# Three operands turned on VectorE and through HBM instead of on TensorE

## The reference, cut to what matters

```python
# hgrn2_chunkwise is the recurrence, h the normed tokens
o_a = rmsnorm(hgrn2_chunkwise(...), hg_norm_g) * silu(g_a)      # the recurrence's gated output
y_a = o_a @ w_branch_a
o_b = fox_attention(...)
y_b = o_b @ w_branch_b
y = gate[:, :, 0] * y_a + gate[:, :, 1] * y_b                   # the mixer's output
x = x + rmsnorm(y @ w_out, mix_post_g)
mem_n = rmsnorm(mem, mem_kv_g)                                  # the memory, normed
k, v = split(mem_n @ w_mkv)
x = x + rmsnorm(mem_cross_attention(rmsnorm(x, mem_pre_g), mem_n, ...), mem_post_g)
```

## Time and profile before

| | |
|---|---|
| median of 3 runs | 1068.75 us (1068.25 to 1068.9) |
| profiled execution | 1069.21 us |
| its span | 1067.2 us |
| PE busy | 1057.5 us, 99% |
| DVE busy | 737.4 us, 69% |
| ACT busy | 596.3 us, 56% |
| HBM read and written | 211.57 MB and 14.68 MB |

### The profile page before, as it was taken

One profiled execution on the slowest core, in us unless ns is written; L12 is line 12 of the kernel. 1 busy time (PEld: TensorE's weight loads), 2 busy tenths in 40 slices (PEclk: granted clock), 3 DMA queues, 4 the chain that ended last, 5 costly groups with the idle time before them and its releaser, 6 DMA issues.

```text
span 1067.2 us, 13290 instructions
## 1 busy us (share of the span) xinstructions
PE 1057.5 (99%) x5158; PEld 889.7 (83%) x5158; DVE 737.4 (69%) x868; ACT 596.3 (56%) x804; POOL 96.1 (9%) x73
## 2 busy tenths in 40 slices
PE   8999999999999999999999999999999999999997
PEld 6888888888888888888888888888989988888886
DVE  5668787785786666467986768657668665867642
ACT  6473677764384645548755545464356557655441
POOL 1900000000000000000545500010000000000000
PEclk9999999999999999999999999999999999999999
DMA  9754899985587777565457844366556346777851
GB/s 351 281 195 158 294 285 307 298 265 195 180 274 247 241 238 233 165 223 180 159 161 225 243 152 158 131 243 218 175 182 216 119 132 218 237 244 240 242 166 40
DMA packets 82831, 227.13 MB, mean 213 GB/s; under 512 B 9377, under 2 KB 28753, under 8 KB 82641
## 3 DMA queue, kind: packets, MB, share of 16 engines
q1 hardware_dynamic: 79344, 214.86, 61.7%
q0 software_dynamic: 3136, 11.23, 2.9%
q10 hardware_dynamic: 288, 0.20, 0.1%
HBM read 211.57 MB, written 14.68 MB: 212 GB/s over the span
## 4 chain that ended last, share of the span: by engine, by line
PE 93%; DVE 3%; ACT 2%; issue 1%; DMA 1%; SPq 0%; DVEq 0%; ACTq 0%
PE ps L734 22%; PE ps L735 22%; PE ps L736 22%; PE ps L773 5%; PE ps L771 5%; PE ps L772 5%; PE ps L868 2%; PE ps L1193 1%; PE ps L1191 1%; PE ps L1192 1%; PE ps L1068 1%; DVE rest L1872 1%; DMA x<-in_x_dram 1%; ACT high L1310 1%; PE ps L830 1%
## 5 line engine op out<-in xcount | busy, mean ns | idle before, releaser
L1872 DVE TENSOR_TENSOR rest<-raw,high 128x2048 fp32r<-128x2048 f32 x131 | 306.7, 2357 | 86.4 <-ACT high L1310 86.0
L734 PE MATMUL ps<-high,xt_high 128*128 128x512 f32 x840 | 330.5, 393 | 0.0
L736 PE MATMUL ps<-high,xt_rest 128*128 128x512 f32 x840 | 327.1, 389 | 0.0
L735 PE MATMUL ps<-rest,xt_high 128*128 128x512 f32 x840 | 327.0, 389 | 0.0
L1310 ACT ACTIVATE high<-raw 128x2048 fp32r<-128x2048 f32 x131 | 248.2, 1913 | 62.2 <-DMA raw<-in_units_dram 62.1
L736 PEld LDWEIGHTS ps<-high,xt_rest 128*128 128x128 f32 x840 | 157.7, 188 | 33.2
L734 PEld LDWEIGHTS ps<-high,xt_high 128*128 128x128 f32 x840 | 157.8, 188 | 31.5
L735 PEld LDWEIGHTS ps<-rest,xt_high 128*128 128x128 f32 x840 | 157.8, 188 | 31.3
L1877 DVE SCALAR_TENSOR_TENSOR rest<-raw,wgain,high 128x512 fp32r<-128x512 f32 x176 | 119.1, 747 | 35.0 <-ACT high L1314 35.0
L1314 ACT ACTIVATE high<-raw,wgain 128x512 fp32r<-128x512 f32 x176 | 110.9, 716 | 8.8 <-DMA raw<-in_units_dram 8.8
L1572 ACT ACTIVATE act<-ps,recips 128x256 f32<-128x256 f32 x44 | 18.4, 470 | 85.1 <-PE ps L736 85.0
(11 more groups left out here) (371 smaller groups left out, 1479.1 us busy)
## 6 DMA issues: line engine op xcount, KB each, us to landing
raw<-in_units_dram SPq DMA_DIRECT2D x350, 512.0 KB, 4.8
gv_turned<-gv_blocked SPq DMA_DIRECT2D x11, 512.0 KB, 6.2
gv_t<-gv_turned SPq DMA_DIRECT2D x44, 128.0 KB, 4.0
turned<-blocked SPq DMA_DIRECT2D x22, 256.0 KB, 5.5
hid_t<-turned SPq DMA_DIRECT2D x88, 64.0 KB, 4.1
raw<-in_units_dram SPq DMA_DIRECT2D x8, 256.0 KB, 6.8
x<-in_x_dram SPq DMA_DIRECT2D x4, 256.0 KB, 7.1
window<-in_c_window_dram POOLq DMA_DIRECT2D x1, 1024.0 KB, 9.6
```

The source lines that it names most:

```text
L734: pe.matmul(out, sh, wh, start=first, stop=False)
L735: pe.matmul(out, sh, wr, start=False, stop=False)
L736: mm = pe.matmul(out, sr, wh, start=False, stop=last)
L1872: vec.tensor_tensor(rest[:, slot, c], raw[:, slot, c], high[:, slot, c].bitcast(F32), ALU.subtract).then_inc(unit_rest, 1)
```

## The change

The operands `o_a`, `mem_n` and `y` are turned by DVE in 32x32 squares and a round trip through HBM. PE's 12 groups of transposes (48 in all) and their PSUM banks go, and with them ACT's and DVE's reads of these banks; ACT and DVE read the landed squares from SBUF instead, with as many elements. Of the six new trips two belong to each operand (one for each token tile of `o_a` and `mem_n`, one for each half of the features of `y`). `OA_SLOT` moves the four groups from steps 30, 31, 32, 33 to steps 31, 32, 34, 35. The `mem_n` groups come after the split of `mk`'s first two units on ACT and DVE, the `y` groups after that of `wout2`'s first two.

```diff
-OA_SLOT = {30 + _g: _g for _g in range(4)}
+OA_SLOT = {31: 0, 32: 1, 34: 2, 35: 3}
...
@@ SyncE, called after the two loads of every unit u
+            def turn(u, at, sems, n, home, landing=None):
+                blocked, stored, landed, scratch = sems
+                if u == at:
+                    sync.wait_ge(blocked, n + 1)
+                    sync.dma_start(scratch[n], home).then_inc(stored[n], 16)
+                if u == at + 1:
+                    sync.wait_ge(stored[n], 16)
+                    src = scratch[n].rearrange("(q i) (r e) -> r i q e", q=4, r=4)
+                    landing = home if landing is None else landing
+                    for r in range(4):
+                        sync.dma_start(landing[32 * r:32 * r + 32, :].rearrange("p (q e) -> p q e", q=4), src[r]).then_inc(landed[n], 16)
+
+            def turn_tokens(u):
+                for tt in range(TT):
+                    turn(u, UNIT["win2"] + 33 + 2 * tt, oa_turn, tt, oa_squares[:, tt, :], hg[:, tt, :])
+                for tt in range(TT):
+                    turn(u, UNIT["brA"] + 9, mem_turn, tt, mem_blocked[:, tt, :])
+                for j in range(2):
+                    turn(u, UNIT["brB"] + 7 + 2 * j, y2_turn, j, y2_blocked[j][:, :])
...
@@ TensorE
-                if u in OA_SLOT:
-                    tt, q = divmod(OA_SLOT[u], 2)
-                    pe.wait_ge(sem("oa_ready"), tt + 1)
-                    transposes(("oa", OA_SLOT[u]), [ho[:, q, tt, c * P:(c + 1) * P] for c in range(4)])
...
-            wait_taken(*(("oa", g) for g in range(4)))
+            pe.wait_ge(sem("oa_rest"), 4)
...
-            token_groups("memn", ...)
...
-            wait_taken(*(("memn", g) for g in range(4)))
+            pe.wait_ge(sem("mem_rest"), 4)
...
-            token_groups("y2", from_y, lambda tt, q: pe.wait_ge(sem("y2_ready"), 2))
...
-            wait_taken(*(("y2", g) for g in range(4)))
+            pe.wait_ge(sem("y2_rest"), 2)
...
@@ ScalarE, step u of win2, behind the gate's tanh
                 if u in OA_SLOT:
-                    group_to_high(("oa", OA_SLOT[u]), at_high[...])
+                    act.wait_ge(oa_turn[2][tt], 64)
+                    act.activation(dst[:, 4 * q:4 * q + 4], src[:, 4 * q:4 * q + 4], ACT.Copy).then_inc(sem("oa_high"), 1)
...
+            split_to(UNIT["mk"] + 2)
+            for tt in range(TT):
+                act.wait_ge(mem_turn[2][tt], 64)
+                for q in range(2):
+                    act.activation(mem_halves(mt_high, tt, q), landed_halves(mem_blocked, tt, q), ACT.Copy).then_inc(sem("mem_high"), 1)
...
             split_to(UNIT["wout2"] + 2)
+            for j in range(2):
+                act.wait_ge(y2_turn[2][j], 64)
+                act.activation(natural(xt_high[:, 4 * j:4 * j + 4, :]), y2_landed(j), ACT.Copy).then_inc(sem("y2_high"), 1)
...
@@ VectorE, gate values of gate 1
+                        if g:
+                            vec.wait_ge(oa_turn[1][1], 16)
...
@@ VectorE, steps 27 and 29
-                    vec.tensor_tensor(o, o, halves(hg[:, tt, :]), ALU.mult).then_inc(sem("oa_ready"), 1)
+                    vec.tensor_tensor(halves(hg[:, tt, :]), o, halves(hg[:, tt, :]), ALU.mult).then_inc(sem("oa_ready"), 1)
+                    vec.wait_ge(sem("oa_ready"), tt + 1)
+                    vec.transpose(oa_squares[:, tt, :]..., hg[:, tt, :]...).then_inc(oa_turn[0], 1)
                 if u in OA_SLOT:
-                    group_to_rest(("oa", OA_SLOT[u]), at_high[at], at_rest[at])
+                    vec.wait_ge(sem("oa_high"), OA_SLOT[u] + 1)
+                    vec.tensor_tensor(dst, src, at.bitcast(F32), ALU.subtract).then_inc(sem("oa_rest"), 1)
...
@@ VectorE, after the memory's norm and before split_to(UNIT["brB"] + 4)
+            for tt in range(TT):
+                vec.wait_ge(sem("mem_normed"), tt + 1)
+                vec.transpose(mem_blocked[:, tt, :]..., mem[:, tt, :]...).then_inc(mem_turn[0], 1)
...
@@ VectorE, for each block j of brB
-                vec.tensor_tensor(y[:, :, c], gate[0][:, :, c], d, ALU.add).then_inc(sem("y2_ready"), 1)
+                vec.tensor_tensor(y2[:, j, :, :, :], fold(gate[0][:, :, c]), fold(d), ALU.add).then_inc(sem("y2_ready"), 1)
+                vec.wait_ge(sem("y2_ready"), j + 1)
+                vec.transpose(y2_blocked[j]..., y2[:, j, :, :, :]...).then_inc(y2_turn[0], 1)
                 if j == 0:
-                    token_groups("memn", mt_high, mt_rest)
                     split_to(UNIT["mk"] + 2)
+                    for n in range(2 * TT):
+                        tt, q = divmod(n, 2)
+                        vec.wait_ge(sem("mem_high"), n + 1)
+                        vec.tensor_tensor(mem_halves(mt_rest, tt, q), landed_halves(mem_blocked, tt, q),
+                                          mem_halves(mt_high, tt, q).bitcast(F32), ALU.subtract).then_inc(sem("mem_rest"), 1)
...
             split_to(UNIT["wout2"] + 2)
+            for j in range(2):
+                vec.wait_ge(sem("y2_high"), j + 1)
+                vec.tensor_tensor(natural(xt_rest[:, k, :]), y2_landed(j), natural(xt_high[:, k, :]).bitcast(F32), ALU.subtract)\
+                    .then_inc(sem("y2_rest"), 1)
```

More of the change, by code:

```diff
@@ L208, in aux_plan @@
                 use(("fo", n - 2))
-    splits("memn")
-    splits("y2")
     splits("mpre")
@@ L348, in build @@
         hg = place("hg", [P, TT, D], F32, area + 16 * KB)
+        oa_squares = place("oa_squares", [P, TT, D], F32, area + 24 * KB)
         gate = [place("gate0", [P, TT, D], F32, area + 8 * KB),
@@ L367, in build @@
         at_high = place("at_high", [P, KC, S], F32R, area + 38 * KB)
-        at_rest = place("at_rest", [P, KC, S], F32R, area + 16 * KB)
+        at_rest = place("at_rest", [P, KC, S], F32R, area)
         fbias = place("fbias", [P, P + S], F32R, area + 62 * KB)
@@ L373, in build @@
         mem = place("mem", [P, TT, D], F32, area + 54 * KB)
+        mem_blocked = place("mem_blocked", [P, TT, D], F32, area + 46 * KB)
+        y2 = place("y2", [P, 2, 4, TT, P], F32, base + 104 * KB)
+        y2_blocked = [place("y2_blocked0", [P, TT * NB], F32, area + 32 * KB), place("y2_blocked1", [P, TT * NB], F32, area + 8 * KB)]
         mt_high = place("mt_high", [P, KC, S], F32R, area + 38 * KB)
@@ L397, in build, with mem_halves, landed_halves, natural @@
         fox_turned = nc.dram_tensor("fox_turned", (4, P, TT * NB), F32, kind="Internal").ap()
+        oa_turn = (sem("oa_blocked"), [sem(f"oa_stored{n}") for n in range(2)], [sem(f"oa_landed{n}") for n in range(2)],
+                    nc.dram_tensor("oa_turned", (2, P, D), F32, kind="Internal").ap())
+        mem_turn = (sem("mem_blocked"), [sem(f"mem_stored{n}") for n in range(2)], [sem(f"mem_landed{n}") for n in range(2)],
+                     nc.dram_tensor("mem_turned", (2, P, D), F32, kind="Internal").ap())
+        y2_turn = (sem("y2_blocked"), [sem(f"y2_stored{n}") for n in range(2)], [sem(f"y2_landed{n}") for n in range(2)],
+                    nc.dram_tensor("y2_turned", (2, P, D), F32, kind="Internal").ap())
+        def mem_halves(ap, tt, q):
+            return ap[:, 4 * q:4 * q + 4, tt * P:(tt + 1) * P].rearrange("p k (n i) -> p k n i", n=4)
+        def landed_halves(ap, tt, q):
+            return ap[:, tt, :].rearrange("p (n k i) -> p k n i", n=4, k=KC)[:, 4 * q:4 * q + 4]
+        def natural(ap):
+            return ap.rearrange("p k (t q i) -> p (k t) q i", t=TT, q=4)
+        def y2_landed(j):
+            return y2_blocked[j][:, :].rearrange("p (q m i) -> p m q i", q=4, m=8)
         gv_turned = nc.dram_tensor("gv_turned", (FB, P, TT * NB), F32, kind="Internal").ap()
@@ L547, in load @@
                 turn_fox(u)
+                turn_tokens(u)
             def turn_fox(u):
@@ L2477, in _ @@
                     o = ho[:, :, tt, :]
-                    vec.tensor_tensor(o, o, halves(hg[:, tt, :]), ALU.mult).then_inc(sem("oa_ready"), 1)
+                    vec.tensor_tensor(halves(hg[:, tt, :]), o, halves(hg[:, tt, :]), ALU.mult).then_inc(sem("oa_ready"), 1)
+                    vec.wait_ge(sem("oa_ready"), tt + 1)
+                    vec.transpose(oa_squares[:, tt, :].rearrange("p (r k i) -> p r k i", r=4, k=KC),
+                                  hg[:, tt, :].rearrange("p (k r i) -> p r k i", k=KC, r=4)).then_inc(oa_turn[0], 1)
                 if u in OA_SLOT:
                     tt, q = divmod(OA_SLOT[u], 2)
-                    at = (slice(None), slice(4 * q, 4 * q + 4), slice(tt * P, (tt + 1) * P))
-                    group_to_rest(("oa", OA_SLOT[u]), at_high[at], at_rest[at])
+                    vec.wait_ge(sem("oa_high"), OA_SLOT[u] + 1)
+                    src = hg[:, tt, :].rearrange("p (q k i) -> p k q i", q=4, k=KC)[:, 4 * q:4 * q + 4]
+                    dst, at = (ap[:, 4 * q:4 * q + 4, tt * P:(tt + 1) * P].rearrange("p k (q i) -> p k q i", q=4) for ap in (at_rest, at_high))
+                    vec.tensor_tensor(dst, src, at.bitcast(F32), ALU.subtract).then_inc(sem("oa_rest"), 1)
```

(17 more changed lines are left out.)

10 lines of the change are left out of this document (2 added, 8 removed).

## The result

The changed kernel takes 1070.65 us, the median of 20 executions (1067.88 to 1073.82), against 1068.97 us for the kernel before in the same rounds (20 executions, 1068.25 to 1069.52). The ratio is 1.0018, 95% interval 1.0013 to 1.0024: slower by 1.7 us, where the forecast was 1068.1. The times also spread far wider than before: sorted, they are one at 1067.9, fourteen between 1069.4 and 1071.3, and five between 1072.8 and 1073.8. The profiled execution took 1070.73 us with a span of 1068.9.

The account below looks back on a forecast made before the run. PE's own instruction stream was taken as the bound, busy 99% of the span. -5.24 + 1.12 + 3.44 + 0 = -0.68 us from 1068.75 gave 1068.1 us, range 1066.0 to 1071.0.

Parts of the forecast that it names:

- What goes: PE's 48 transposes of o_a, mem_n and y, with the cost behind each group: 5.24 us off PE.
- Step 28: Unit 28 of win2: DVE's square transpose at step 27 delays fox_scale, so PE waits 1.12 us; bounds 0 and 1.3.
- The cover at step 29: DVE's square transpose at step 29: 1.6 us of cover, nothing lost; without it another 1.2 us.
- Step 35: Last group of o_a stands behind ACT's last tanh; PE waits 3.44 us before brA; bounds 2.8 and 4.2.
- rival (c): PE's clock falls in the wait before brA: 1.7 us lost, or 3.5 if low twice as long; chance 0.15.
- The memory: mem_n's trip before mk: last rest just in time, 0 us lost, almost no cover left; bounds 0 and 2.
- Rival (b): Memory lands late, mk starts 0.5 to 2 us late: 1068.6 to 1070.1 us; chance 0.20.
- Other edits at nothing: Loads held back on SP, y's trips, copies and subtractions: no cost; with cover gone, each 0 to 2 us.

Follow-up runs that it names:

- all waits mended: Changed kernel with OA_SLOT at steps 31 to 34, o_a's square transposes behind fox_scale, memory's norm and squares before brA's second block is gated: 1063.54 us, ratio 0.9950.
- the one with the memory early: Changed kernel with the memory's norm and square transposes on DVE moved ahead of the gating of brA's second block: 1070.11 us, ratio 1.0010.
- the one kept at work: Changed kernel with 15 extra f32 matmuls on PE ahead of the wait for the last rest before brA: 1068.38 us, ratio 0.9999.
- the two with the memory early: Changed kernel with memory's norm and squares before brA's second block is gated, with the change's slots (1070.11 us) or slots 31 to 34 (1064.72 us).
- the second experiment: Changed kernel with OA_SLOT at steps 31 to 34 and DVE's square transposes of o_a behind fox_scale of steps 28 and 30: 1065.06 us, ratio 0.9968.

## Why the prediction was wrong

- **What goes** (5.24 us): right. With all waits mended the gain is 5.5 us.
- **Step 28** (1.12 us): right. 1.13 in the profile, 1.2 between two runs that differ in it alone. The cover at step 29 held.
- **Step 35** (3.44 us): the wait was right, 3.53. The term was too small because it counted the wait and not what stands behind it. This is the step that failed: the sum put the price of the last group of `o_a` at the idle time, and gave the fall of the clock as rival (c) a chance of 0.15. In the kernel as changed both profiles have it, and so has the one with the memory early. Of 32 times one alone, 1067.88 with a mean clock of 1.000, is where the forecast 1068.1 had them all, and the next is 1069.23; five of the others have a mean clock of 0.999, which leaves room for only some 3 us at the lower level, so in how many executions it fell, and how far, is read from the times and not shown for each. Its size was in the text (1.7 to 3.5 us); it measured 2.6 in the profile, 2.3 between the changed kernel and the one kept at work, and 1.9 between the two with the memory early. It is also what the prediction named as a sign of being wrong, a clock below 1.00 after 706 us. The trace before had no idle time of PE over 1 us between 11 us and its tail; the tail itself has a fall, which the prediction did not use (its row stands under this list). The row of the Trainium skill, TensorE: Matmul & The Clock Gate, section Why this matters for your kernels, that warns of idle gaps between bursts of matmuls, did bear on the case and deserved the larger chance. The runs agree with it at the wait before `brA` (3.28 us of idle time in the profile). They show a fall behind shorter ones too: 1.93 us of idle time with the late memory of the second experiment (2.1 lost) and 1.78 at the start of one execution. Behind 1.54 (1.8 lost), and behind 0.53 and 0.74 before `mk`, there was none.
- **The memory** (0, bounds 0 to 2): the working was right for the profiled execution to 0.2 us, but a slack of 0.1 us is none. In the second experiment's profile the trip took 2.4 us longer; the early memory takes 0.5 us off the changed kernel's median, and none of its 11 executions is above 1071.3, where the changed kernel had 9 of 32. A wait for the memory with a second fall of the clock behind it is shown in one profile, of the second experiment; that it makes the changed kernel's slow executions is argued. Rival (b) was not instead of the forecast but beside it.
- **Other edits at nothing**: right. SP held back loads by up to 4.7 us (that of `mk`'s last unit, issued at 749.07 where PE's finish let it go at 744.39), and no unit came late.
- **The direction.** The forecast was 0.7 us faster by the sum, and it was that near to nothing only because 5.24 us of gain stood against 4.56 of waits. With (c) as a term, -5.24 + 1.12 + 3.44 + 2.6 = +1.9, the forecast would have been 1070.7 from the 1068.75 that it started from, against 1070.65 measured. The range held the time, 0.35 us under its upper end and by the rival that made that end, not by the forecast's own path.

The tail of the trace before (the clock by stretch):

```profile
1066.00:1067.00 1.00, 0.00 (x0) 0.00 (x0) 0.00 (x0) 0.00 (x0) 0.00 (x0) 0.63 0.29 99
```

PE's last matmul there ends at 1061.64, and the granted clock is 1.00 up to 1066. So the fall while PE idles was already in that trace, some 4.6 us after PE stopped, which is longer than the 3.44 us of the forecast's wait; in the changed kernel's tail it took 2.7 us (1063.32 to 1066.0).

## What to carry to other kernels

An operand that leaves the busiest engine is a gain only down to the next thing that this engine waits for: follow the last piece of the operand through every in-order queue it stands in, and compare it with the moment that the busy engine takes it. Behind a wait of TensorE the clock can fall: here waits of 2.1 to 3.5 us cost another 1.5 to 2.6 us by it. Price both, and if the wait can't go, shorten it or fill it with matmuls. A slack is to be compared with how much a DMA round trip varies: here it was 0.1 us, and the memory's trip took 14.1 us in one profile and 16.5 in another.

## What the runs showed of the hardware that I had not expected

- The clock's fall does not come at a fixed distance from the idle time. With a wait of the same length it came while PE idled (changed kernel, 707.6) or 1.5 us after PE was back at work (the same kernel again, 711.4), and behind a wait of 2.1 us it came 0.9 us after (the second experiment). The work done at the lower level lasted 5.6, 3.1, 3.4, 3.4 and 3.4 us in five profiles (the changed kernel, the kernel before with the late slots, the changed kernel again, the second experiment, the changed kernel with the memory early). This alone spreads the times by more than 1 us; the kernel before spread by 1.3 us in its 20 executions beside the changed kernel's.
- A plain f32 matmul of 128 columns took 0.22 us on PE and is recorded twice, while a transpose of the same f32 square takes 1.66 / 16 = 0.10 us.
- Stores of 512 KB of the same form landed after 2.7 us for `o_a` and after 5.8 and 8.0 us for the memory's and `y`'s first in the changed kernel's profile, the latter two with a store or unit loads issued beside them.
